# Where matrix operands begin in SBUF: xh and xl 64 bytes, op_hi and op_lo 96 bytes behind multiples of 256

## What is computed

```python
proj = xn @ w_in
y = jax.nn.sigmoid(xn @ w_gate[i]) * (merge_heads(branches[i]) @ w_branch[i])
hdn = xn @ w_up
h = h + 0.5 * swiglu(rmsnorm_2(h, ffn1_norm[l]), ffn1_w_gate[l], ffn1_w_up[l], ffn1_w_down[l])
z = rmsnorm_2(h, mix_norm[l]) @ w_in[l]
h = h + jnp.concatenate([y_a, y_b, y_c, y_d], axis=-1) @ w_out[l]
```

## Time and profile before

| what | before |
|---|---|
| median of three executions | 3053.2 us |
| profiled execution, first to last instruction | 3051.8 us |
| TensorE matmul busy | 3019.8 us (99%), 14622 records |
| GpSimd busy | 2180.6 us (71%) |
| VectorE busy | 1407.5 us (46%) |
| ScalarE busy | 736.2 us (24%) |
| mean share of the DMA engines | about 30%, 89 GB/s |

### The profile page before, as it was taken

How to read it: one execution, slowest core, us unless ns; L and a number is a source line. 1 busy time by engine, 2 the same in 40 slices (tenths; PEclk the granted TensorE clock), 3 DMA queues, 4 the chain that set the end, 5 groups by cost and what they waited for, 6 DMA issues and landing times.

```text
span 3051.8 us, 38797 instructions
## 1 busy us (share of the span) xinstructions
PE 3019.8 (99%) x14622; PEld 2459.3 (81%) x14622; DVE 1407.5 (46%) x2133; ACT 736.2 (24%) x1466; POOL 2180.6 (71%) x2524
## 2 busy tenths in 40 slices
PE   9999999999999999999999999999999999999998
PEld 7776777888888888887788888888888887888886
DVE  5467556777157321476732212622223767422214
ACT  3433222222021110354411101311003444111003
POOL 6665678988788777754487777877777454877775
PEclk9999999999999999999999999999999999999999
DMA  5322223333333333312133332333333221333332
GB/s 162 79 67 63 77 80 90 100 98 98 99 94 104 101 97 97 92 51 59 56 100 98 97 104 92 97 97 97 97 97 96 57 54 49 104 97 97 104 97 83
DMA packets 469203, 272.86 MB, mean 89 GB/s; under 512 B 20799, under 2 KB 465137, under 8 KB 469017
## 3 DMA queue, kind: packets, MB, share of 16 engines
q1 hardware_dynamic: 466904, 267.22, 29.7%
q10 hardware_dynamic: 2112, 3.17, 0.3%
HBM read 268.21 MB, written 2.12 MB: 89 GB/s over the span
## 4 chain that ended last, share of the span: by engine, by line
PE 87%; DVE 3%; ACT 1%; issue 0%; DVEq 0%
PE bank L726 17%; PE bank L727 17%; PE bank L735 17%; PE bank L1268 7%; PE bank L1267 7%; PE bank L1275 7%; PE bank L848 2%; PE bank L856 1%; PE bank L849 1%; PE bank L773 1%; PE bank L1438 1%; PE bank L774 1%; DVE arena L2349 1%; PE bank L778 1%; PE bank L1120 1%; PE bank L883 1%
## 5 line engine op out<-in xcount | busy, mean ns | idle before, releaser
L683 POOL TENSOR_TENSOR wl<-raw,wh 128x256 fp32r<-128x256 f32 x2016 | 1622.0, 835 | 285.7 <-PE bank L735 180.6
L676 POOL TENSOR_SCALAR wh<-raw 128x1024 fp32r<-128x1024 f32 x504 | 562.2, 1115 | 562.9 <-PE bank L727 171.7
L726 PE MATMUL bank<-xh,wh 128*128 128x512 f32 x1552 | 610.7, 393 | 0.0
L727 PE MATMUL bank<-xl,wh 128*128 128x512 f32 x1552 | 604.3, 389 | 0.0
L2349 DVE TENSOR_TENSOR arena<-bank,nrm 128x512 f32<-128x512 f32 x236 | 152.4, 686 | 541.7 <-PE bank L735 541.4
L735 PE MATMUL bank<-xh,wl 128*128 128x512 f32 x1552 | 390.6, 391 | 0.0
L2349 DVE TENSOR_TENSOR arena<-arena 128x512 f32<-128x512 f32 (+1 forms) x373 | 336.9, 910 | 64.6 <-ACT arena L2049 11.7
L726 PEld LDWEIGHTS bank<-xh,wh 128*128 128x128 f32 x1552 | 291.7, 188 | 62.6 <-issue 2.1
L735 PEld LDWEIGHTS bank<-xh,wl 128*128 128x128 f32 x1552 | 289.9, 188 | 64.6 <-issue 4.6
L727 PEld LDWEIGHTS bank<-xl,wh 128*128 128x128 f32 x1552 | 291.6, 188 | 60.3 <-issue 1.2
L726 PE MATMUL bank<-arena_rounded,wh 128*128 128x512 f32 x824 | 321.7, 390 | 1.0 <-DVE arena L2349 1.0
(11 more groups left out here) (366 smaller groups left out, 4151.8 us busy)
## 6 DMA issues: line engine op xcount, KB each, us to landing
raw<-in_ffn_w_gate SPq DMA_DIRECT2D x176, 256.0 KB, 3.1
raw<-in_ffn_w_up SPq DMA_DIRECT2D x176, 256.0 KB, 3.1
raw<-in_ffn_w_down SPq DMA_DIRECT2D x176, 256.0 KB, 3.0
raw<-in_w_in SPq DMA_DIRECT2D x158, 256.0 KB, 3.1
raw<-in_w_up SPq DMA_DIRECT2D x88, 256.0 KB, 3.1
raw<-in_w_gate SPq DMA_DIRECT2D x64, 256.0 KB, 2.9
raw<-in_w_out SPq DMA_DIRECT2D x48, 256.0 KB, 2.9
raw<-in_w_down SPq DMA_DIRECT2D x44, 256.0 KB, 3.0
```

The source lines that it names most:

```text
L676: pool.tensor_scalar(wh[:, s, :], raw[:, s, :], 1.0, 0.0, ALU.mult, ALU.add).then_inc(split, 1)
L683: ins = pool.tensor_tensor(wl[:, s, c], raw[:, s, c], wh[:, s, c].bitcast(F32), ALU.subtract)
L726: pe.matmul(psum, cols(wh, i), xhi, start=(i == 0), stop=False)
L727: ins = pe.matmul(psum, cols(wh, i), xlo, start=False, stop=False)
```

## The change

Two unused tensors of 64 and 32 bytes per partition are put ahead of `xh` and of `op_hi`, and the unused `between` shrinks by 96 bytes, so that everything from `wh` on stays where it was. By the rule of placement above, `xh` and `xl` are then at 64, and `op_hi` and `op_lo` at 96. Not named by the change, but moved by it too: `raw` goes from 0 to 96, `eps` too, `const` from 32 to 128, `ident16` and `mask16` from 64 to 160. `arena`, `h`, `wh`, `wl`, `ones` and `nrm` keep their addresses. Each engine has the same instructions in the same order.

```diff
     assert nc.sbuf_base % 256 == 0, nc.sbuf_base % 256
 
+    sb("before_x", [P, 16])
     xh, xl = sb("xh", [P, DC, S], F32R), sb("xl", [P, DC, S], F32R)
+    sb("before_op", [P, 8])
     op_hi, op_lo = sb("op_hi", [P, 4, S], F32R), sb("op_lo", [P, 4, S], F32R)
 
     raw = sb("raw", [P, 2, PIECE])
...
     ident16, mask16 = sb("ident16", [P, P], BF16), sb("mask16", [P, P + 2], BF16)
-    sb("between", [P, 40])
+    sb("between", [P, 16])
     assert nc.sbuf_base % 256 == 0, nc.sbuf_base % 256
     wh, wl = sb("wh", [P, 2, PIECE], F32R), sb("wl", [P, 2, PIECE], F32R)
```

## The result

Three executions of the changed kernel took 3068.3 to 3071.23 us, median **3068.36 us**, against 3053.2 us before: the ratio is 1.0055, with a 95% interval from 1.0041 to 1.0068. The profiled execution spans 3067.0 us at a granted clock of 0.998, 15.2 us more than before. I had forecast no change, 3053.2 us. The measured time still lies inside my range of 3046 to 3082 us; that is luck, as the last part shows, because nothing that the range was widened for took place.

What follows compares the result with a forecast made beforehand. TensorE, busy 3019.8 of 3051.8 us, was taken as the bound. All terms were priced 0, so 3051.8 us of span plus 1.4 us for the median gave 3053.2 us, range 3046 to 3082 us.

Steps and rivals of the forecast that it cites:

- Matmuls from moved operands: TensorE's 7704 matmuls reading xh, xl, op_hi or op_lo: priced 0 from float32 rows, with ends of +-103 us.
- my own decision point: 0.8 ns a matmul from moved operands, 6.1 us in all: about what a measurement can tell from no change.
- constant to the tenth of a ns: Said of the extra each TensorE matmul costs over its columns, 13.4 ns with 512 columns.
- the pace hangs neither on the source nor on what the other engines do in SBUF: TensorE starts the same 443 matmuls in three 100 us stretches with different sources and different VectorE load.
- Rival A: TensorE reads by 256-byte blocks; a shifted operand covers one more, 1.7 ns on each of 7704 matmuls: 3066 us; chance 22%.
- D's smaller form: GpSimd's reads of raw 20% slower, only the densest stretch (the convolution's weights) pays: +15 us, 3068 us.
- Rival C: Float32r operands beginning at the same place pay 13.4 ns for meeting; shifting one removes it: at most −103 us, 2950 us; 15%.
- Rival B: TensorE operands starting off a boundary pay the start extra twice or in part: up to +103 us, 3156 us; chance 8%.
- Rival D: GpSimd becomes the bound, reading raw at 96 at least 22% slower: up to +180 us if everywhere; chance 3%.
- GpSimd, VectorE, ScalarE and constants at 0: Engine operations on moved tensors, GpSimd's reads of raw at 96, and moved constants, identity and mask: each priced 0.
- The DMAs at 0: DMAs writing raw at 96: priced 0, hidden by TensorE's hold on GpSimd, even with a landing of about 3.7 us.
- The sign that would show it: Forecast wrong if xh or op_hi pace differs from the large buffer's by 0.8 ns; boundary not 256 if 64 and 96 differ.

## Why the prediction was wrong, point by point

- **"Matmuls from moved operands", priced 0: the step that failed.** The 7704 matmuls that were put at 0 took 14.2 us more (+11.6, +6.0 and −3.4 us in the table above). Of my 6936 with 512 columns, 24 that read `op_hi` and `op_lo` have 256, which changes nothing. The 0 was taken from float32 rows, "as these rows are nearest in kind". They are of another kind. In them a difference of 128 (the large buffer against `ones`) leaves 1.7 ns over the columns of a pass; the same difference in float32r costs 46 cycles over the columns, 19 ns. The later layouts also put `ones` at 0, 64, 160 and 192, and the distances from one float32 matmul of a norm to the next stay at 428 to 432 ns, where they were 428 to 434: float32 moves by at most 6 ns in its two passes. For float32r the measured price is +2.2 ns for 512 columns at a difference of 64, +6.7 ns at 96 by the chain (7.0 by the mean step), and about −5 ns for 256 moving columns at 192. All three were within the +-13.4 ns that I had kept as bounds, and my own decision point was 0.8 ns.
- **What the rows before could not have told:** in the kernel before every float32r operand has difference 0, so that "constant to the tenth of a ns" was one point of a curve, not a sign of flatness. That "the pace hangs neither on the source nor on what the other engines do in SBUF" was right for what it compared, since both sources stand at the same place. I read it as if it spoke of places.
- **Rival A (blocks of 256 bytes, 3066 us)** had nearly the time, and at 64 bytes nearly the pace (228.4 ns forecast, 228.9 measured), and the wrong mechanism. It wanted one price for 64 and 96 (they are 2.2 and 6.7 ns), a rise for the 256-column matmuls too (they fell), 1.7 ns a matmul when the weights move (it was 6.6 ns), and the same loss with everything at 64 (there was none). Its nearness to 3068.4 us is luck, a sum of unlike terms, +11.6, +6.0 and −3.4 us. So is it luck that my range held the time: its upper end came from A and from D's smaller form, and neither happened.
- **Rival C (the two operands meet)** had right what counts, the two places taken together, and for 512 columns the wrong sign: beginning at the same place is the cheapest case tested, not the dear one. Only with 256 moving columns does leaving it pay. The Trainium skill ("TensorE: Matmul & The Clock Gate", Back-to-back issue gap) gives N/2.4 + 2.5 ns at the full clock for an isolated matmul, which makes 215.8 ns for 512 columns; no layout came under 226.7. What the Trainium skill says on the same page (Step-by-step: what each phase is for) of two independent read ports, one for the streaming operand and one for the weight load, does not foretell what was measured: as the two places were set against each other, the step moved from 544 to 562 cycles.
- **Rival B (start paid twice)** would have made 240 ns; the dearest step measured is 234.3. **Rival D** did not happen: TensorE waits for GpSimd once, for 0.3 us. The row of that wait in the changed kernel (us in all, times, longest):

```profile
PE bank L876 <- POOL wh L678: 0.3, 1, 0.3
```

- **GpSimd, VectorE, ScalarE and constants at 0** were right: 1.0001 for the kernel that shifts `raw` and the constants alone. **The DMAs at 0** too. The landing of the pieces of `in_ffn_w_gate` and `in_ffn_w_up` went from 3.1 us to 3.2, and to at most 3.3 where `raw` and the constants alone were moved and where `raw` was at 64. By the beats that the Trainium skill ("DMA: Bandwidth & Descriptors", How a descriptor splits into AXI transactions) counts, I had an estimate of 3.7 us; the traces show at most a third of that rise.
- **The sign that would show it** served: "the pace from `xh` or `op_hi` differs from that of the large buffer by 0.8 ns or more" is what the profile showed at once. "If 64 and 96 bytes differ from one another, the boundary that counts is not 256" led the wrong way. They do differ, and 256 is still the period; what was wrong was the thought of a boundary.

The same sums account for the slowdown with the weights at 64: 4554 steps from the large buffer rise by 6.5 ns (+29.8 us), 5887 from `xh` and `xl` by 5.9 (+35.0), 998 from `op_hi` and `op_lo` by 5.4 (+5.4), and the 256-column ones fall by 2.5 us in all: +67.7 us, against 65.3 us of span.

**Still open.** Why 512 columns take 32 cycles more even at difference 0, and why the curve has this shape, was not settled: steps come in patterns of two or three values (226, 229 and 232 ns at 64), which suggests a beat between two accesses, but that was only thought, not tested. Nor is it settled which two reads meet. In the kernel before, nearly every weight load (`PEld`) of a float32r matmul starts together with the matmul ahead of it, as here:

```profile
1500.25 0.39 PE L774 MATMUL bank<-xl,wh 128*128 128x512 f32 x1
1500.25 0.19 PEld L778 LDWEIGHTS bank<-xh,wl 128*128 128x128 f32 x1
```

So the stationary operand being read while a moving one streams is that of the next matmul. In nearly every pair of neighbours here both stationary operands have the same place, so that a matmul's own pair can't be told from the pair of neighbours.

Places between the multiples of 16 listed, and for 512 columns differences of 112, 144, 176 and 240, weren't tried, so a cheaper one isn't excluded. Nor was a layout that gives the 256-column matmuls a difference of 192 while those of 512 columns keep 0; both kinds read the same tensors here. No version that was run beats the kernel before.

## What to carry to other kernels

Where TensorE is the bound and works in float32r, work out for each pair of operands where the moving one and the stationary one begin, and take the difference modulo 256 bytes: keep it at 0 for 512 moving columns. An alignment assert on both sides does that, and one shared offset does as well; paddings that shifted one against the other cost 0.2 to 2.4% here. And a price that no row of a profile shows should not be put at nothing from rows of another data type: rows that all stand at one place show nothing of what other places cost.

## What the runs showed of the hardware that I had not expected

- The step between float32r matmuls of 512 columns depends on the difference of the two operands' places modulo 256 bytes: 226.7 ns at 0, 228.9 at 64, 231.7 at 16, 234.3 at 160, at a granted clock of 1.00. It does not depend on the place itself: with all at 64 it is 226.7 ns again. Float32 matmuls against `ones` moved by at most 6 ns in 433, over two passes.
- With 256 moving columns another difference is the cheapest of those tested. The mean steps are 119.8 ns at a difference of 0, 114.9 at 192 (`xh` at 64, weights at 0) and 113.3 at 192 for the large buffer's values (weights at 192); at 128 they are 118.6 to 118.8. So the same difference of 192 that adds 16 cycles to a matmul of 512 columns takes 12 to 16 from one of 256.
- The VectorE operation on the large buffer took 686 ns before and with everything at 64, and GpSimd's operation that reads `raw` took 835 ns with it at 0 and 837 with it at 96. ScalarE's operation that writes `xh` took 725 ns before and 724 with it at 64. A dependence on these places was found on TensorE alone.
